# Finer waits ahead of the attention scores, a moved gate, and two smaller TensorE edits in a hybrid decoder step

## The reference, cut to what matters

```
q = einsum('bsr,re->bse', rms_norm(q_down, q_norm_g), w_uq)        # 256 wide
ckv = rms_norm(ckv_raw, kv_norm_g)                                 # 128 wide
q_lat = einsum('bshd,rhd->bshr', q_nope, w_uk)
s = einsum('bqhr,bkr->bhqk', q_lat, ckv) + einsum('bqhd,bkd->bhqk', q_rope, krope)
s = where(kpos <= qpos, s * MLA_SCALE, NEG_INF)
o_lat = einsum('bhqk,bkr->bqhr', softmax(s), ckv)
mla_out = einsum('bshr,rhd->bshd', o_lat, w_uv).reshape(B, S, 256)
mixed = concatenate([..., mla_out * silu(mla_gate), ...])
```

## Time and profile before

| | |
|---|---|
| median of 3 runs | 3778.59 us (3778.5 to 3778.81) |
| the profiled execution: time | 3779.04 us |
| its span, first to last instruction | 3777.2 us |
| granted TensorE clock, mean | 0.986 |
| TensorE busy (matmul) | 3590.7 us, 95% |
| VectorE busy | 1686.6 us, 45% |
| ScalarE busy | 1387.7 us, 37% |

### The profile page before, as it was taken

One profiled execution on the slowest core, in us unless ns is written; L12 is line 12 of the kernel. 1 busy time (PEld: TensorE's weight loads), 2 busy tenths in 40 slices (PEclk: granted clock), 3 DMA queues, 4 the chain that ended last, 5 costly groups with the idle time before them and its releaser, 6 DMA issues.

```text
span 3777.2 us, 74999 instructions
## 1 busy us (share of the span) xinstructions
PE 3590.7 (95%) x31016; PEld 2634.5 (70%) x31016; DVE 1686.6 (45%) x4348; ACT 1387.7 (37%) x3767; POOL 163.4 (4%) x284
## 2 busy tenths in 40 slices
PE   4999999999999999999879999999999999999997
PEld 2868687776868677586547686868777686766863
DVE  1535445454544535345325454544535454353542
ACT  1333334233343433534323333342433435244342
POOL 0010100000000000000000000000000000000000
PEclk8999999999999999999889999999999999999998
DMA  6434342524334143241433433334152332423313
GB/s 224 127 122 140 119 132 69 170 81 136 99 108 141 48 170 92 75 130 42 152 124 94 152 103 130 121 119 130 59 176 92 119 101 76 161 70 119 94 34 119
DMA packets 319598, 431.85 MB, mean 114 GB/s; under 512 B 26846, under 2 KB 276652, under 8 KB 319100
## 3 DMA queue, kind: packets, MB, share of 16 engines
q1 hardware_dynamic: 297052, 376.15, 30.6%
q0 software_dynamic: 11648, 41.95, 3.1%
q10 hardware_dynamic: 10560, 8.95, 0.8%
HBM read 405.22 MB, written 32.26 MB: 116 GB/s over the span
## 4 chain that ended last, share of the span: by engine, by line
PE 87%; ACT 6%; issue 3%; DVE 3%; ACTq 1%; DVEq 1%; DMA 0%; POOL 0%; SPq 0%; POOLq 0%
PE bank L702 79%; PE bank L706 7%; ACT hT L2082 1%; DVEq L1343 1%; DVE ml L1642 1%; ACT Q L2242 0%; ACTq L2221 0%; ACT L2222 0%; ACT PT L2357 0%; ACT Sm L2317 0%; ACT qr L2241 0%; ACT PT L2166 0%; ACT Q L2240 0%; DVE bon L1467 0%; DMA kv<-in_w_mem_v 0%
## 5 line engine op out<-in xcount | busy, mean ns | idle before, releaser
L702 PE MATMUL bank<-hT,win 128*128 128x256 f32 (+3 forms) x7168 | 1603.7, 378 | 4.5 <-ACT hT L2082 4.5
L702 PEld LDWEIGHTS bank<-hT,win 128*128 128x128 f32 (+1 forms) x7168 | 1259.3, 186 | 218.8 <-issue 41.6
L702 PE MATMUL bank<-kv,Q 96*128 96x512 f32 (+3 forms) x640 | 277.1, 531 | 11.1 <-ACT mix L2104 11.1
L1642 DVE TENSOR_REDUCE ml<-bank 128x1 f32<-128x512 f32 (+3 forms) x320 | 195.4, 611 | 128.8 <-PE bank L702 117.9
L706 PEld LDWEIGHTS bank<-cst,Sm 128*128 128x128 f32 x1344 | 153.1, 140 | 140.6 <-issue 65.3
L706 PE MATMUL bank<-cst,Sm 128*128 128x128 f32 x1344 | 215.3, 281 | 26.5 <-ACT Sm L2317 18.8
L702 PE MATMUL bank<-wout,mix 128*128 128x512 f32 x512 | 231.6, 600 | 8.0 <-ACT hT L2082 6.5
L2317 ACT ACTIVATE Sm<-bank,ml 128x512 f32<-128x512 f32 (+3 forms) x320 | 199.7, 624 | 80.3 <-DVE ml L1647 71.5
L702 PEld LDWEIGHTS bank<-wout,mix 128*128 128x128 f32 x512 | 95.0, 191 | 122.8 <-issue 120.7
L2104 ACT ACTIVATE mix<-bank 128x256 f32<-128x256 f32 x128 | 49.1, 383 | 332.1 <-PE bank L702 332.1
L2211 ACT ACTIVATE mix<-bank 128x512 f32<-128x512 f32 (+1 forms) x68 | 39.6, 596 | 303.1 <-PE bank L702 303.1
(11 more groups left out here) (475 smaller groups left out, 5743.4 us busy)
## 6 DMA issues: line engine op xcount, KB each, us to landing
win<-in_w_in SPq DMA_DIRECT2D x176, 1024.0 KB, 5.3
wout<-in_w_out SPq DMA_DIRECT2D x68, 512.0 KB, 7.6
xin<-out_xres SPq DMA_DIRECT2D x32, 1024.0 KB, 7.5
PT<-in_w_out SPq DMA_DIRECT2D x32, 512.0 KB, 3.7
XX<-in_w_out SPq DMA_DIRECT2D x32, 512.0 KB, 4.1
out_xres<-xin SPq DMA_DIRECT2D x16, 1024.0 KB
win<-in_w_in SPq DMA_DIRECT2D x16, 896.0 KB, 4.9
win<-in_w_in SPq DMA_DIRECT2D x16, 640.0 KB, 4.6
```

Of the source, the lines that this page charges most:

```text
L702: return pe.matmul(out, lhsT, rhs, start=start, stop=stop, skip_group_check=True)
L1642: v.tensor_reduce(top, bank[:, 0:w], AX, MAX)
```

## The change

Four edits. (1) In `attention` the four waits ahead of the first scores are taken apart: chunks 0 and 1 wait only for the keys, chunk 2 (now in bank 7) for tile 23 to be read out, chunk 3 (now in bank 6) for tile 24, chunk 4 (bank 5) for the last RWKV output. (2) ScalarE computes the gate's tanh behind the attention's last copy and no longer ahead of its first exponential. (3) VectorE adds the two planes of squares of `qd` before TensorE sums over partitions, so `latent_norms` has two products and no longer three. (4) The inverse sums are turned by four transposes and no longer by four products with the identity.

```diff
@@ score_bank
-            return (0, 1, 6, 7, 5)[c % 5]
+            return (0, 1, 7, 6, 5)[c % 5]
@@ latent_norms (TensorE)
                 mm(PP[7][:, 0:B.n], ones, sqn[:, 0, 0:B.n])
-                mm(PP[7][:, T:T + B.n], ones, sqn[:, 1, 0:B.n], True, False)
-                mm(PP[7][:, T:T + B.n], ones, sqn[:, 2, 0:B.n], False, True).then_inc(s_sqd.h, 1)
+                mm(PP[7][:, T:T + B.n], ones, sqn[:, 1, 0:B.n]).then_inc(s_sqd.h, 1)
@@ attention (TensorE)
                 pe.wait_ge(s_kvd.h, s_kvd.at(B.it, 1))
                 pe.wait_ge(s_krt.h, s_krt.at(B.ip, 2))
-                pe.wait_ge(s_pa.h, s_pa.at(B.ip, NTILES - 2))
-                pe.wait_ge(s_yr.h, s_yr.at(B.ip, 4))
                 for c in range(5):
+                    if c == 2:
+                        pe.wait_ge(s_pa.h, s_pa.at(B.ip, NTILES - 3))
+                    elif c == 3:
+                        pe.wait_ge(s_pa.h, s_pa.at(B.ip, NTILES - 2))
+                    elif c == 4:
+                        pe.wait_ge(s_yr.h, s_yr.at(B.ip, 4))
                     scores(c)
@@ attention_out (TensorE)
                     for i in range(4):
-                        last = mm(PP[5][:, i * P:(i + 1) * P], inv64[:, 2 * i:2 * i + 2, :], ident)
+                        last = tr(PP[5][:, i * P:(i + 1) * P], flat3(T3)[:, i * P:(i + 1) * P], P)
                     last.then_inc(s_uv.h, 1)
@@ rwkv_prepare (VectorE)
-                v.tensor_tensor(sqn[:, 1:3, 0:n], qd[:, :, 0:n], qd[:, :, 0:n], MULT).then_inc(s_sq.h, 1)
+                v.tensor_tensor(sqn[:, 1:3, 0:n], qd[:, :, 0:n], qd[:, :, 0:n], MULT)
+                drain()
+                v.tensor_tensor(sqn[:, 1, 0:n], sqn[:, 1, 0:n], sqn[:, 2, 0:n], ADD).then_inc(s_sq.h, 1)
                 rotate_keys(B)
@@ block (ScalarE)
                     take_tile(B, 24, mix[:, 5, :])
-                    gate(mix[:, 4:6, :], Kt)
...
                         if c + 1 < n:
                             probs(c + 1)
                         take(c)
+                    gate(mix[:, 4:6, :], Kt)
```

## The result

The changed kernel takes 3747.71 us (median of 6 runs, 3746.8 to 3748.3) against 3778.7 us for the kernel before in the same session. The ratio is 0.9916, 95% interval 0.9904 to 0.9929: 31 us less, where 27.9 were forecast. The interval reaches from 27 to 36 us less, so the times alone can't tell the excess of 3 us from noise; the traces have to show it. The forecast of 3751 us is 3.3 us too high.

What follows compares the result with a forecast made beforehand. TensorE, its matmuls busy 95% of the span, was taken as the bound. Gains of 13.7 + 0 + 6.9 + 7.3 = 27.9 us from 3779.04 gave 3751.1, on the median's scale 3750.7, stated as 3751 us; range 3747 to 3763.

Steps and rivals of the forecast that it cites:

- given back at the first turn: Rival, chance 0.10: the wait for the first exponential grows by what the scores' earlier start saves; 3764.8 us.
- The gap: TensorE's stand between tile 24 and the first scores: 0.85 us a block, 0.91 in the two 264-column blocks.
- so the whole chain moves forward with it: Mask, row maximum and first exponential follow only the first score; mask 0.50 us behind it, exponential wait stays 0.43 us.
- The term was 13.7 us: Forecast gain from removing the gap ahead of the first scores: 14 x 0.85 + 2 x 0.91 us.
- upper bound of 14.6: Most the separated waits ahead of the first scores could gain, in us: a gap of 0.91 in all blocks.
- 0.07 us of slack: ScalarE's idle time left before the first block's first exponential, had the gate stayed while the scores start earlier.
- 6.9 forecast: At the latent norms, one product with ones of 0.433 us gone in 16 blocks: 6.9 us, bounds 0 and 6.9.
- 7.3 forecast: At the inverse sums, four transposes take 0.44 us instead of 0.89: 0.45 us a block, 7.3 us in all.
- Counting starts and not record lengths: At the inverse sums, records overlap, so costs were taken from start to start: transposes 0.109 us each.
- 20 in a block instead of 16: Transpose count in the clock rival, chance 0.03: clock falls to 1.2 GHz after the attention, 7.1 us per block, 3864 us.
- there is little to be had from the clock: The clock is granted in full outside start, middle and end, TensorE at 2.4 GHz through the blocks; no gain forecast.
- the rule on transposes: Transposes don't count as busy TensorE, so more could cost clock; answered by 16 in a row without a fall, cost none.

Runs made afterwards that it cites:

- e1: The waits ahead of the first scores taken apart and banks 6 and 7 exchanged, alone on the kernel before: 3765.25 us, ratio 0.996.
- e9: The changed kernel with the joint wait ahead of the first scores and the old banks put back: 3764.0 us, ratio 0.9959.

## Why the prediction was right in kind and short in size

**Edit 1.** Right in its mechanism: the wait was for a bank wanted three chunks later, it went as a whole, chunks 2 to 4 wait for nothing new, nothing was given back at the first turn. The gap was sized rightly: 0.84 in the trace against 0.85. The first step that failed is the sentence "so the whole chain moves forward with it", with the mask "still" 0.50 us behind the scores. It starts 0.42 us behind them, because the first product behind the wait was slower than the same one in a running stream: in the kernel before its first record was 0.35 us long and the next started 0.18 us behind it, in the changed kernel 0.27 and 0.11 us; the ten records together last 3.26 us and now 3.19. VectorE, ScalarE and the first turn all get these 0.07 us too, in each block, 1.1 us in all. The term was 13.7 us; the traces have 13.7 + 1.1 = 14.8, above its upper bound of 14.6, and alone the edit measured 14.6.

**Edit 2.** Right: nothing alone (0.9998) and nothing undone in the changed kernel. With 0.07 us of slack forecast in the first block the trace shows none left, and none lacking. At its new place it leaves ScalarE 3.25 us of idle time in the block shown.

**Edit 3.** 6.9 forecast, 6.9 measured. VectorE came out in time, as worked out: it ends the work ahead of L1436 at 1183.62, and the last product with ones ends at 1183.68.

**Edit 4.** 7.3 forecast, 7.3 measured. Counting starts and not record lengths was right. The remark of the Trainium skill ("TensorE: Matmul & The Clock Gate", Part 4: PE-mode transpose) on transposes and the clock, weighed in the prediction, had no consequence here: with four transposes more in each block the changed kernel's clock fell in no block, in two traces. (The prediction's "20 in a block instead of 16" counts only those behind the attention; over the run the traces have 2720 transposes against 2656.)

**The sum.** It stood on "outside the start, the middle and the end ... it is granted in full", and so on "there is little to be had from the clock", read from the earlier trace rows. That is the second step that failed, a term put at nothing. A slice there is 94 us long and 9 means 90% or more, so a fall of a few us can't be seen in it; the stretches cut around 245 and 2089 us show 0.89 and 0.58. The prediction's answer to the rule on transposes leaned on the same slices. In the changed kernel's two traces both falls are gone, worth 1.69 and 1.57 us. The direct terms as the traces have them, 13.7 + 1.1 + 6.9 + 7.3 = 29.0 us, and 3.3 us of clock give 32.3, against 32.2 between the two profiled executions' spans (other single differences of under 1 us nearly cancel); the medians of the runs differ by 31.0.

The prediction took the clock to be full and forecast nothing of it, so that the falls went away was luck. It isn't shown that the idle time in the narrow first blocks made it fall: places with the same idle time kept the clock, e1 alone gave in its medians nothing beyond its direct terms, and e9 lost a fall without having edit 1. What decides a single fall stays open.

The low end of the range had no term under it either: with the upper bound of edit 1, 14.6 us, the sum gives 3750, and 3747 allowed for 3 us more without saying from where.

The gain was forecast with the right sign and for the right reasons. The size was short by 1.1 us for the mask, which every block of the traces shows, and by about 2 us for the clock, which the traces show (3.3 us) but the times of the runs can't tell from noise.

## What to carry to other kernels

Look in the wait list for a wait that comes exactly once per iteration and ask which buffer it is for and when that buffer is first wanted; a joint wait ahead of a loop often belongs to its third or fourth step. The same question found 7 to 8 us more in the output projection. Count the gain from start to start: it is the idle time of the profile plus the latency that a running TensorE hides (0.84 us for 0.68), and a little for the engines behind it (0.07 us here). Read the clock in stretches of a few us around the narrow phases, not in the page's slices. And before a table of runs is taken to show a cause, divide it by every other edit in which the runs differ: here two divisions gave the same 2 against 13.

## What was not expected of the hardware

The granted clock drops to half inside the steady part of the kernel: in the kernel before behind a stretch of 10 us with TensorE busy for 7.28, but not behind one with 7.25 in the other layer, nor with 7.99 in the changed kernel; each drop cost 1.6 to 1.7 us. A fall in the output projection came while TensorE was busy throughout (4.00 of 4 us at 0.57), so the idle time nearest to a loss can lie some us ahead of it. The first product behind a wait brought its consumer 0.07 to 0.08 us later than the same product in a running stream.
